# Latent attention scores from 96 rows: two full passes and a 32-row rest for pairs of tiles

## The reference

```python
c_q = rmsnorm(z[:, cq]); c_kv = rmsnorm(z[:, ckv]); k_rope = rope(z[:, kr])   # 256, 256, 32 columns
q = (c_q @ w_uq).reshape(512, 8, 64 + 32);  q[..., 64:] = rope(q[..., 64:])
kv = (c_kv @ w_ukv).reshape(512, 8, 64 + 64)
k = concat(kv[..., :64], k_rope shared by the 8 heads)                        # 96 wide
o_mla = softmax(q @ k.T / sqrt(96)) @ kv[..., 64:]
```

## Time and profile before

| | |
|---|---|
| median of 3 runs | 1208.68 us (1206.12 to 1209.07) |
| the profiled execution's own time | 1210.87 us |
| its span | 1209.0 us |
| mean granted TensorE clock | 0.993 |
| busy: PE, DVE, ACT, POOL | 98%, 73%, 50%, 48% |
| share of PE in the chain that ended last | 93% |

### The profile page before, as it was taken

How to read it: one execution, slowest core, us unless ns; L and a number is a source line. 1 busy time by engine, 2 the same in 40 slices (tenths; PEclk the granted TensorE clock), 3 DMA queues, 4 the chain that set the end, 5 groups by cost and what they waited for, 6 DMA issues and landing times.

```text
span 1209.0 us, 16359 instructions
## 1 busy us (share of the span) xinstructions
PE 1189.2 (98%) x5672; PEld 974.2 (81%) x5672; DVE 882.8 (73%) x1356; ACT 600.4 (50%) x986; POOL 582.3 (48%) x371
## 2 busy tenths in 40 slices
PE   8999999999999999999999999999999999999997
PEld 7887678888888888888887776888888888888886
DVE  4657867656779776889856677776658778767896
ACT  5345766743544344435423466666444544344443
POOL 1014554622865676565510145537047665766462
PEclk8999999999999999999999999999999999999999
DMA  5521110134234322431324201102342334223402
GB/s 160 157 70 62 45 24 30 53 87 147 76 92 139 106 90 87 137 105 36 105 58 121 70 27 44 36 18 88 86 159 89 87 105 140 88 81 111 140 13 92
DMA packets 128132, 104.56 MB, mean 86 GB/s; under 512 B 5514, under 2 KB 107956, under 8 KB 128052
## 3 DMA queue, kind: packets, MB, share of 16 engines
q1 hardware_dynamic: 127840, 103.50, 28.9%
q10 hardware_dynamic: 84, 0.02, 0.0%
q0 software_dynamic: 128, 0.00, 0.0%
HBM read 99.84 MB, written 2.10 MB: 84 GB/s over the span
## 4 chain that ended last, share of the span: by engine, by line
PE 93%; DVE 2%; POOL 2%; DMA 1%; ACT 1%; issue 1%; SPq 0%; POOLq 0%; DVEq 0%; ACTq 0%
PE bank L1520 82%; PE bank L1590 3%; PE bank L1618 3%; PE bank L1561 2%; DMA stage<-in_w_in 1%; POOL rs L621 1%; PE bank L1538 1%; DMA xin<-in_x 1%; DVE k_pack L1177 0%; PE bank L1698 0%; PE bank L1690 0%; PE bank L1547 0%; PE bank L1753 0%; DVE w_lo L1066 0%; POOL e_x L630 0%
## 5 line engine op out<-in xcount | busy, mean ns | idle before, releaser
L1520 PE MATMUL bank<-u_hi,w_hi 128*128 128x512 f32 x760 | 299.3, 394 | 0.3
L1520 PE MATMUL bank<-u_hi,w_lo 128*128 128x512 f32 x760 | 296.1, 390 | 0.0
L1520 PE MATMUL bank<-u_lo,w_hi 128*128 128x512 f32 x760 | 295.9, 389 | 0.0
L750 ACT ACTIVATE w_hi<-stage 128x1024 fp32r<-128x1024 f32 (+2 forms) x141 | 136.4, 977 | 225.8 <-DMA stage<-in_w_up 92.2
L1066 DVE TENSOR_TENSOR w_lo<-stage,w_hi 128x1024 fp32r<-128x1024 f32 (+2 forms) x116 | 136.6, 1187 | 57.6 <-ACT w_hi L750 57.2
L1520 PEld LDWEIGHTS bank<-u_hi,w_hi 128*128 128x128 f32 x760 | 142.8, 188 | 31.0 <-issue 2.5
L1520 PEld LDWEIGHTS bank<-u_hi,w_lo 128*128 128x128 f32 x760 | 142.7, 188 | 30.3
L1520 PEld LDWEIGHTS bank<-u_lo,w_hi 128*128 128x128 f32 x760 | 142.9, 188 | 28.3
L750 ACT ACTIVATE w_hi<-b 128x1024 fp32r<-128x1024 f32 x84 | 89.0, 1059 | 129.8 <-PE bank L1520 88.8
L1520 PE MATMUL bank<-w_hi,quad_hi 128*128 128x512 f32 x392 | 152.6, 389 | 0.0
L1520 PE MATMUL bank<-w_hi,quad_lo 128*128 128x512 f32 x392 | 152.5, 389 | 0.0
(11 more groups left out here) (237 smaller groups left out, 2293.6 us busy)
## 6 DMA issues: line engine op xcount, KB each, us to landing
stage<-in_w_up SPq DMA_DIRECT2D x64, 512.0 KB, 4.1
b<-in_w_down SPq DMA_DIRECT2D x56, 512.0 KB, 3.5
stage<-in_w_in SPq DMA_DIRECT2D x32, 512.0 KB, 3.9
stage<-in_w_out SPq DMA_DIRECT2D x16, 512.0 KB, 3.6
stage<-in_w_down SPq DMA_DIRECT2D x8, 512.0 KB, 3.4
xin<-in_x SPq DMA_DIRECT2D x4, 512.0 KB, 7.1
stage<-in_w_ukv SPq DMA_DIRECT2D x4, 512.0 KB, 3.5
out<-yout SPq DMA_DIRECT2D x8, 256.0 KB, 2.4
```

The lines of the kernel that those rows point to most:

```text
L750: last = nc.scalar.activation(hi(w_hi, s)[:, :, d:d + n], st(r)[:, :, f:f + n], ACT.Copy)
L1520: mm = nc.tensor.matmul(acc, a, b, start=first and t == 0 and m == 0, stop=last and t == len(terms) - 1 and m == 2)
```

## The change

An exact sum over 96 rows needs three products of 96 rows, 288 in all. They are laid out as 128 + 128 + 32. First the rotary part of the query is summed on DVE, so that a query has 96 rows, no longer 128. Then:

- first pass: rows 0 to 95 low half of the query, rows 96 to 127 high half of its rotary part, against plain key high (64 rows) and rotary key high (twice 32);
- second pass: the plain query's high half twice (rows 0 to 63 and 64 to 127), against plain key high and plain key low;
- rest, 32 rows: rotary query high against rotary key low. The rest of an even tile runs in rows 64 to 95 (from a new buffer `q_third`), that of the next, odd tile in rows 96 to 127 (from the query buffer), one behind the other into two banks (`third_pair`). So an even tile's scores end one step later.

What produces the operands changes with it: three DVE operations, four ACT copies and two POOL differences for a query; four ACT copies for two for a pair of keys; a rotary key one step earlier, with DMAs of half the size. The fill order becomes q2 in step 16, kp1 in 18, v3 in 19. The fourth sub-norm's power and `stat_b` move behind the step's other work. Lastly, 12 and 5 transposes of the identity are added at the start, in front of the first two and the last two of x's first four turns.

```diff
-    for use, n in (..., ("kp0", 10), ("q0", 11), ("v2", 12), ("q1", 14), ("v3", 16), ("q2", 17)):
+    for use, n in (..., ("kp0", 10), ("q0", 11), ("v2", 12), ("q1", 14), ("q2", 16), ("kp1", 18), ("v3", 19)):
...
-        if hd % 2 == 0:
+        if hd % 2 == 0 and hd:
             fill[n + 2].append((f"kp{hd // 2 + 1}", range(KC)))
...
@@ SP
                         sp.wait_ge(krb_hi_made, val(krb_hi_made, l, 1))
-                        sp.wait_ge(krb_lo_made, val(krb_lo_made, l, 1))
-                        sp.dma_start(k_pack[NOPE:P, 1, :, :].bitcast(F32), k_pack[NOPE:P, 0, :, :].bitcast(F32)).then_inc(krb_copied, 16)
+                        sp.dma_start(k_pack[NOPE:P, 1, 0, :].bitcast(F32), k_pack[NOPE:P, 0, 0, :].bitcast(F32)).then_inc(krb_copied, 16)
...
@@ POOL, query_low
-                nc.gpsimd.tensor_tensor(q_tile(hd)[1], tmp_y[:, 0, :], q_tile(hd)[0].bitcast(F32), ALU.subtract
+                low, high = q_tile(hd)
+                nc.gpsimd.tensor_tensor(low[0:NOPE], tmp_y[0:NOPE, 0, :], high[0:NOPE].bitcast(F32), ALU.subtract
+                                        ).then_inc(q_nope_low, 1)
+                pool.wait_ge(q_nope_low, val(q_nope_low, l, hd + 1))
+                nc.gpsimd.tensor_tensor(low[NOPE:QK], tmp_y[NOPE:QK, 0, :], q_third[hd % 2][NOPE:QK, :].bitcast(F32), ALU.subtract
                                         ).then_inc(q_lo_made, 1)
+                pool.wait_ge(q_lo_made, val(q_lo_made, l, hd + 1))
...
-                    if r == 0 and 0 <= g < DIFF_HEADS:
+                    if (r == 0 and 0 <= g < DIFF_HEADS - 1) or (r == 1 and g == DIFF_HEADS - 1):
                         power(l, MISC_AT[f"sub{g}_c"], 3 + g, rs)
@@ ACT, gen
-                        nc.scalar.activation(k_pack[0:NOPE, 2 * (j % 2) + p, 0, :],
+                        for half in range(2):
+                            last = nc.scalar.activation(k_pack[0:NOPE, 2 * (j % 2) + p, half, :],
...
-                    act.wait_ge(*read_out(l, use))
+                    act.wait_ge(q_roped, val(q_roped, l, hd + 1))
...
-                    nc.scalar.activation(q_tile(hd)[0], tmp_y[:, 0, :], ACT.Copy).then_inc(q_hi_made, 1)
+                    low, high = q_tile(hd)
+                    for dst, rows in ((high[0:NOPE], slice(0, NOPE)), (high[NOPE:P], slice(0, NOPE)),
+                                      (q_third[hd % 2][NOPE:QK, :], slice(NOPE, QK)), (low[QK:P], slice(NOPE, QK))):
+                        last = nc.scalar.activation(dst, tmp_y[rows, 0, :], ACT.Copy)
+                    last.then_inc(q_hi_made, 1)
...
-                    if n == DSTEPS - 4:
+                    if n == DSTEPS - 5:
@@ DVE, gen
-                    nc.vector.tensor_tensor(tmp_y[:, 0, :], b[:, :], tabq, ALU.mult).then_inc(freed(use), 1)
+                    nc.vector.tensor_tensor(tmp_y[0:QK, 0, :], b[0:QK, :], tabq[0:QK, :], ALU.mult)
+                    nc.vector.tensor_tensor(tmp_y[NOPE:QK, 1, :], b[QK:P, :], tabq[QK:P, :], ALU.mult).then_inc(freed(use), 1)
+                    dve.wait_ge(*read_out(l, use))
+                    nc.vector.tensor_tensor(tmp_y[NOPE:QK, 0, :], tmp_y[NOPE:QK, 0, :], tmp_y[NOPE:QK, 1, :], ALU.add
+                                            ).then_inc(q_roped, 1)
...
-                    if n == DSTEPS - 3:
+                    if n == DSTEPS - 4:
                         dve.wait_ge(krb_hi_made, val(krb_hi_made, l, 1))
-                        nc.vector.tensor_tensor(k_pack[NOPE:P, 0, 1, :], krf[NOPE:P, :],
+                        nc.vector.tensor_tensor(kr_lo[NOPE:P, :], krf[NOPE:P, :],
@@ PE, scores
-                pe.wait_ge(sc_free, val(sc_free, l, e - 2))
-                three(SC_BANKS[e % 3][:, :], ..., True, True).then_inc(sc_done, 1)
+                if qt % 2:
+                    third_pair(l, n - 1)
+                else:
+                    pe.wait_ge(sc_free, val(sc_free, l, e - 2))
+                q = slice(qt * P, (qt + 1) * P)
+                nc.tensor.matmul(SC_BANKS[e % 3][:, :], q_tile(hd)[0][:, q], k_pack[:, hd % 4, 0, :], start=qt % 2 == 0, stop=False)
+                mm = nc.tensor.matmul(SC_BANKS[e % 3][:, :], q_tile(hd)[1][:, q], k_pack[:, hd % 4, 1, :], start=False, stop=qt % 2 == 1)
+                if qt % 2:
+                    mm.then_inc(sc_done, 1)
+
+            def third_pair(l, n):
+
+                hd, qt = divmod(n - DSTEPS, TT)
+                e = DSTEPS + n
+                pe.wait_ge(sc_free, val(sc_free, l, e - 1))
+                for m, tile in enumerate((q_third[hd % 2], q_tile(hd)[0])):
+                    rows, q = slice(NOPE + m * ROPE, NOPE + (m + 1) * ROPE), slice((qt + m) * P, (qt + m + 1) * P)
+                    mm = nc.tensor.matmul(SC_BANKS[(e + m) % 3][:, :], tile[rows, q], kr_lo[rows, :], start=m == 1, stop=m == 0)
+                    if m == 0:
+                        mm.then_inc(sc_done, 1)
...
@@ PE, start
+            keep_busy(12)
...
-            for j in range(4):
+            for j in range(2):
+                first_turn(j)
+            keep_busy(5)
+            for j in range(2, 4):
                 first_turn(j)
...
@@ PE, step n (stat_b of the fourth sub-norm now behind `turn`)
-                    if r == 3 and 0 <= g < DIFF_HEADS:
+                    if r == 3 and 0 <= g < DIFF_HEADS - 1:
                         stat_b(l, MISC_AT[f"sub{g}_b"], 3 + g)
...
                     if n:
                         turn(l, n - 1)
+                    if r == 3 and g == DIFF_HEADS - 1:
+                        stat_b(l, MISC_AT[f"sub{g}_b"], 3 + g)
```

More of the change, by code:

```diff
@@ L77, in fillers @@
             n += 2
-    for use, n in (("v0", 8), ("v1", 9), ("kp0", 10), ("q0", 11), ("v2", 12), ("q1", 14), ("v3", 16), ("q2", 17)):
+    for use, n in (("v0", 8), ("v1", 9), ("kp0", 10), ("q0", 11), ("v2", 12), ("q1", 14), ("q2", 16), ("kp1", 18), ("v3", 19)):
         fill[n].append((use, range(KC)))
@@ L275, in trunk @@
     tmp_y = place("tmp_y", [P, 2, SEQ], F32)
+    q_third = [None, place("q_third1", [P, SEQ], F32R, at_byte[0])]
     rb = place("rb", [P, SEQ], F32)
+    kr_lo = place("kr_lo", [P, SEQ], F32R, at_byte[0])
     krf = place("krf", [P, SEQ], F32)
@@ L279, in trunk @@
     hid_lo.append(place(f"hid_lo{FC - 1}", [P, SEQ], F32R, at_byte[0] - 2 * kb))
+    q_third[0] = place("q_third0", [P, SEQ], F32R, at_byte[0] + 4 * C_TABK)
     consts = place("consts", [P, C_W], F32)
@@ L343, in trunk @@
         v_hi_made, k_hi_made = counter("v_hi_made", TT), counter("k_hi_made", MLA_HEADS)
-        q_hi_made, q_lo_made = (counter(n, MLA_HEADS) for n in ("q_hi_made", "q_lo_made"))
+        q_roped, q_hi_made, q_nope_low, q_lo_made = (counter(n, MLA_HEADS)
+                                                     for n in ("q_roped", "q_hi_made", "q_nope_low", "q_lo_made"))
         sc_done, sc_free = (counter(n, 2 * DSTEPS + MSTEPS) for n in ("sc_done", "sc_free"))
@@ L585, in _ @@
                         sp.wait_ge(krb_hi_made, val(krb_hi_made, l, 1))
-                        sp.wait_ge(krb_lo_made, val(krb_lo_made, l, 1))
-                        sp.dma_start(k_pack[NOPE:P, 1, :, :].bitcast(F32), k_pack[NOPE:P, 0, :, :].bitcast(F32)).then_inc(krb_copied, 16)
+                        sp.dma_start(k_pack[NOPE:P, 1, 0, :].bitcast(F32), k_pack[NOPE:P, 0, 0, :].bitcast(F32)).then_inc(krb_copied, 16)
                         sp.wait_ge(misc_done, val(misc_done, l, MISC_AT[f"pv{DIFF_HEADS - 1}"] + 1))
                         for p in (2, 3):
-                            sp.dma_start(k_pack[NOPE:P, p, :, :].bitcast(F32), k_pack[NOPE:P, 0, :, :].bitcast(F32)).then_inc(krb_copied, 16)
+                            sp.dma_start(k_pack[NOPE:P, p, 0, :].bitcast(F32), k_pack[NOPE:P, 0, 0, :].bitcast(F32)).then_inc(krb_copied, 16)
             for tt in range(TT):
@@ L806, in gen @@
                     for p in range(2):
-                        nc.scalar.activation(k_pack[0:NOPE, 2 * (j % 2) + p, 0, :],
-                                             bank[BANK[use]][p * NOPE:(p + 1) * NOPE, :], ACT.Copy
-                                             ).then_inc(k_hi_made, 1)
+                        for half in range(2):
+                            last = nc.scalar.activation(k_pack[0:NOPE, 2 * (j % 2) + p, half, :],
+                                                        bank[BANK[use]][p * NOPE:(p + 1) * NOPE, :], ACT.Copy)
+                        last.then_inc(k_hi_made, 1)
                 elif use[0] == "q":
                     hd = int(use[1:])
-                    act.wait_ge(*read_out(l, use))
+                    act.wait_ge(q_roped, val(q_roped, l, hd + 1))
                     act.wait_ge(sc_done, val(sc_done, l, 2 * DSTEPS + TT * (hd - 1) if hd else 2 * (DSTEPS - TT)))
-                    nc.scalar.activation(q_tile(hd)[0], tmp_y[:, 0, :], ACT.Copy).then_inc(q_hi_made, 1)
+                    low, high = q_tile(hd)
[3 more added lines that the diff above has]
+                    last.then_inc(q_hi_made, 1)
             def pv_out(l, g):
@@ L1176, in gen_low @@
```

(15 more changed lines are left out.)

## The result

The changed kernel takes 1265.2 us (median of 5 runs, 1264.8 to 1268.1), the one before 1207.3 (5 runs): ratio 1.048, 95% interval 1.0462 to 1.0498. It is slower, as forecast, but by 58 us and not by 20, and beyond the stated range of 1204 to 1243.

A forecast was written before the change was run, and what follows sets the result against it. PE, busy 98%, was taken to bound the kernel, with side engines setting the pace in places. Per layer 2.0 + 4.4 + 0 + 5.1 = 11.5, twice 23, less 3.0: +20, so 1229 us, range 1204 to 1243.

The forecast's parts named there:

- named signs: PE idle 2 to 4 us at steps 13, 17, 18; steps 23 to 39 over 48 us; full pass 0.4 after pair.
- The start: Kernel start, 8.61 to 15 us: filler transposes keep the clock at 2.4 GHz, -3.0 us, bounds -3.2 and +1.1.
- The pairs: Latent scores on PE: 32 lone pairs, +2 us while PE sets the pace, 0 in the sum; bounds -7.3 and +5.1.
- my 0.29 for the switch: Latent scores on PE: going into and out of row groups costs two tiles 0.39 - 0.10 = 0.29 us more.
- The query's surcharge: Hand-over DVE, ACT, DVE: 1.4 + 1.5 = 2.9 us more for each query.
- the first: Steps 11 to 13: late row constant delays PE's transposes by 2.0 us per layer, bounds 0 and 3.4.
- the second: Steps 15 to 18: q1 and q2 work makes the value product 4.4 us late per layer, bounds 1.3 and 5.8.
- the third: Steps 19 to 21: the 1.01 us wait goes but kp1 has four copies; 0 per layer, between -1.0 and +1.4.
- Steps 22 to 39: Five queries and two k pairs add 16.7 us, DVE idle takes 11.6; 5.1 us remain per layer, between 0 and 9.
- Rival 4: Every wait adds, and the clock falls behind each long gap: 1245 us and over, chance 0.08.

The follow-up runs named there:

- side_only: The changed kernel with three full passes for each tile's scores and no row-group pair: 1267.2 us, ratio 1.0479 to the kernel before.
- query_keys: The kernel before with all new query work and new key copies, old fill order, three full passes: 1264.2 us against 1208.1, ratio 1.0449.
- harmless_parts: The kernel before with the start's filler transposes and the fourth sub-norm's move: 1208.8 us against 1206.9, ratio 1.0012.
- one_copy: The changed kernel with three full passes and one ACT copy of each query for four: 1231.6 us, ratio 1.0197 to the kernel before.
- late_copies: The changed kernel with a second scratch tile, ACT's copies and POOL's differences of queries except q0 one step later: 1254.5 us, ratio 1.0382 to before.
- clock_filler: The changed kernel with 8 filler transposes ahead of the turn in steps 13, 15, 17, 20 and 21: 1270.6 us, ratio 1.0519 to before.

## Why the prediction missed the size

- **The direction and the cause** were right: the side work in the hand-over from DVE to ACT to DVE makes the kernel slower, with or without the pairs (side_only, query_keys). Of the named signs only some came. Steps 23 to 39 got longer, with gaps on PE, and the full pass follows the pair after 0.43 us. But PE was to stand idle for 2 to 4 us before the transposes of steps 13 and 17 and the values of step 18; it stood for 0.34, 0.63 and 0.85, and for 3.06 before the transposes of step 16, which had no term.
- **The start**, put at -3.0 us: it is 2.0 in the trace and 1.7 in the time. That it came near is in part luck. The half clock in the earlier trace rows belonged to one execution; five of seven other traces with the old start don't have it, and are 1.9 to 2.4 us early at tile 2 as well.
- **The pairs**, counted at 0 (+2, bounds -7.3 and +5.1): alone they cost 3.5 to 4.4 us, near the upper bound; beside the side work nothing that can be told. All of the extra time falls on the odd tile, and my 0.29 for the switch was 0.40.
- **The query's surcharge**, put at 2.9 us: ACT's copies of a query start 0.63 apart and not 0.53 (2.55 us for four), +0.4 a query. No row of the prediction shows the 0.53. In after the copies of a key pair, which read PSUM, come 0.54 apart (four in 2.17 us), and those of a query, which read SBUF, don't. (The prediction also has +1.6 for the copies in one sentence and 1.5 in the sum, and two DMAs for three; neither matters.)
- **The places**: the first was put at 2.0 us and lost 3.4, the second at 4.4 and lost 9.4, the third at 0 and lost 1.3. Steps 22 to 39 were put at 5.1 and lost 12.2 (1.8 of it from tile 20 to tile 21, as much as the move of the fourth sub-norm costs there in layer 1 of harmless_parts), and 2.8 came in behind them, where I had no term. The second place and steps 22 to 39 lie outside their bounds (5.8 and 9). In the second, the sum had a whole round of 3.4 for q1 and only 1.0 for the round of q2.
- **The step that failed** is the sum for steps 22 to 39: "DVE's idle time there is 48.0 - 36.39 = 11.6, and in the best case all of it is used." I took idle time as room that a surcharge fills first, and subtracted all of it. The runs show that it isn't filled. In the 58 us window of after DVE is idle for 14.8 us, more than the 11.6 of before, and DVE's waits for ACT's high halves in the two windows grew with the load from 8.3 to 13.1 us, seven times each (rows below). Idle time of an engine that hands every tile to another and back is for the most part waiting for that other. Of 16.7 us of surcharge 12.2 reached PE, against 5.1. And where the other pieces have taken what slack there was, a piece costs its full time (one_copy: 34 to 36 us for 31).
- **The clock** was at nothing in the sum. Rival 4 had it, at 1245 and over with a chance of 0.08, and came nearest. After misses 25 us of clock (a span of 1263.4 at 0.980), the kernel before 4 at its median of 0.997. From 164.7 to 174.3 us a higher clock only made PE wait longer. On the chain it stretches PE by some 5 us more than before, and by the 0.6 us per us of the repeated runs the 21 us would be 13. So it carries some 5 to 13 of the 58 us, an estimate with the direction not shown.
- **What stays open**: that share of the clock, and which mix of load and order makes the last 46 us that late_copies leaves.

DVE's waits for ACT, 180 to 228 us in before and 194 to 252 us in after (us in total, times, longest):

```profile
DVE pt_lo L1130 <- ACT pt_hi L782: 8.3, 7, 2.2
...
DVE pt_lo L1143 <- ACT pt_hi L790: 13.1, 7, 2.3
```

## What to carry to other kernels

Fewer passes on the engine that sets the pace pay only if making their operands costs the others less than what they have left. What they have left is not the sum of their idle time. So add one piece at a time to the old kernel, and expect the last to cost its full length even if the first cost under a half of it (here 31 us of copies cost 13.5 first and 34 to 36 last). A lone row-group pair between full passes loses to the two passes that it saves (0.17 us for two tiles here). When the shares of busy time look the same after a change, read the chain and the waits. And before a stretch of low clock in one trace is priced, look whether a second execution has it: the one at the start did not come back in five of seven.

## What the runs showed of the hardware

- A ScalarE copy of 512 columns from SBUF takes 0.63 us with 32, 64 or 128 rows, across partitions or not, and the next starts 0.64 us later; copies from PSUM with 64 rows follow each other after 0.54.
- At the start TensorE ran nothing but transposes from 1.7 to 9.5 us, and the granted clock was 1.00 in all eleven traces with the filler. The Trainium skill (TensorE: Matmul & The Clock Gate, Part 4: PE-mode transpose) says that transposes don't count as busy; the start speaks against it. Eight transposes ahead of each of five turns (clock_filler) left 47.8 us of half clock, as many as without; small matmuls in the 3 us gap before 164.7 kept the clock at 1.00 there.
- Whether the clock falls differs from one execution to the next: 0.50, 0.66, 0.69 and five times 1.00 from 9 to 14 us with the same start.
- Filler that holds the clock gained nothing in the one stretch where a late producer stood behind it: PE reached the same wait at the same time (174.34 and 174.36 us).
